# Reading the columns of every 352-column product from last to first

## What is computed

```python
def trunk(x, b_conv, b_h, c_conv, p):
    for l in range(DEPTH):                      # DEPTH = 2
        hn = rmsnorm(x, p['norm_mix_pre'][l])
        if l % 2 == 0:
            m, v, bc, bh = mixer_even(hn, ...)  # h @ w_in (1024 x 2048), gating, LRU, @ w_out (1024 x 1024)
        else:
            m, cc = mixer_odd(hn, ...)          # h @ w_in (1024 x 3072), convolution, @ w_out (1024 x 1024)
        x = x + rmsnorm(m, p['norm_mix_post'][l])
        hn = rmsnorm(x, p['norm_ffn_pre'][l])
        f = jnp.square(jax.nn.relu(hn @ p['mlp_up'][l])) @ p['mlp_down'][l]
        x = x + rmsnorm(f, p['norm_ffn_post'][l])
```

## Time and profile before

| | |
|---|---|
| Three runs | 2157.94 us median (2157.59 to 2158.12) |
| Profiled execution, first to last instruction (its span) | 2155.1 us, mean granted clock 0.999 |
| TensorE (PE) busy | 2146.0 us, 13,496 records |
| Weight loads (PEld) busy | 2135.0 us, 13,496 records |
| VectorE (DVE) busy | 908.0 us |
| ScalarE (ACT) busy | 652.9 us |
| GpSimd (POOL) busy | 100.1 us |

### The profile page before, as it was taken

How to read it: one execution, slowest core, us unless ns; L and a number is a source line. 1 busy time by engine, 2 the same in 40 slices (tenths; PEclk the granted TensorE clock), 3 DMA queues, 4 the chain that set the end, 5 groups by cost and what they waited for, 6 DMA issues and landing times.

```text
span 2155.1 us, 31488 instructions
## 1 busy us (share of the span) xinstructions
PE 2146.0 (100%) x13496; PEld 2135.0 (99%) x13496; DVE 908.0 (42%) x1414; ACT 652.9 (30%) x1105; POOL 100.1 (5%) x127
## 2 busy tenths in 40 slices
PE   9999999999999999999999999999999999999998
PEld 9999999999999999999999999999999999999998
DVE  8766367323322322334953333493223223322336
ACT  6673355202301310333511112453013103202332
POOL 2000000000000000000043231000000000000000
PEclk9999999999999999999999999999999999999999
DMA  5111422111111111141311114222111111111142
GB/s 165 35 41 40 139 88 72 50 40 49 50 42 47 49 50 40 49 135 44 120 50 47 43 50 139 67 84 59 42 48 50 49 40 50 50 42 48 50 140 81
DMA packets 208410, 138.65 MB, mean 64 GB/s; under 512 B 6000, under 2 KB 204784, under 8 KB 208272
## 3 DMA queue, kind: packets, MB, share of 16 engines
q1 hardware_dynamic: 207552, 135.51, 20.6%
q10 hardware_dynamic: 720, 1.13, 0.1%
HBM read 119.22 MB, written 17.40 MB: 63 GB/s over the span
## 4 chain that ended last, share of the span: by engine, by line
PE 99%; ACT 1%; DMA 0%; DVE 0%; issue 0%; DVEq 0%; ACTq 0%
PE ps L698 32%; PE ps L700 32%; PE ps L699 32%; PE ps L773 1%; PE ps L801 0%; PE ps L729 0%; PE ps L720 0%; DMA w_all_raw<-in_w_in_even_dram 0%; PE ps L716 0%; PE ps L784 0%; PE ps L760 0%; ACT L1074 0%; ACT L1030 0%; ACT lru L1030 0%; ACT lru L1032 0%; ACT gelu L1074 0%
## 5 line engine op out<-in xcount | busy, mean ns | idle before, releaser
L698 PE MATMUL ps<-x_hi,w_all 128*128 128x352 f32 x2304 | 747.0, 324 | 0.0
L700 PE MATMUL ps<-x_hi,w_all 128*128 128x352 f32 x2304 | 739.1, 321 | 0.0
L699 PE MATMUL ps<-x_lo,w_all 128*128 128x352 f32 x2304 | 739.1, 321 | 0.0
L698 PE MATMUL ps<-h_hi,w_all 128*128 128x352 f32 x1728 | 556.2, 322 | 0.0
L700 PE MATMUL ps<-h_hi,w_all 128*128 128x352 f32 x1728 | 555.2, 321 | 0.0
L699 PE MATMUL ps<-h_lo,w_all 128*128 128x352 f32 x1728 | 555.2, 321 | 0.0
L698 PEld LDWEIGHTS ps<-x_hi,w_all 128*128 128x128 f32 x2304 | 432.4, 188 | 2.7
L699 PEld LDWEIGHTS ps<-x_lo,w_all 128*128 128x128 f32 x2304 | 432.4, 188 | 2.2
L700 PEld LDWEIGHTS ps<-x_hi,w_all 128*128 128x128 f32 x2304 | 432.3, 188 | 0.0
L876 ACT CAST w_all<-w_all_raw 128x1024 fp32r<-128x1024 f32 x166 | 173.5, 1045 | 525.1 <-DMA w_all_raw<-in_mlp_down_dram 324.8
L698 PEld LDWEIGHTS ps<-h_hi,w_all 128*128 128x128 f32 x1728 | 324.5, 188 | 0.3 <-DVE h_lo L1452 0.3
(11 more groups left out here) (201 smaller groups left out, 1416.0 us busy)
## 6 DMA issues: line engine op xcount, KB each, us to landing
w_all_raw<-in_mlp_up_dram SPq DMA_DIRECT2D x60, 512.0 KB, 3.9
w_all_raw<-in_mlp_down_dram SPq DMA_DIRECT2D x60, 512.0 KB, 3.8
x_save<-f SPq DMA_DIRECT2D x9, 1408.0 KB, 6.0
x_old<-x_save SPq DMA_DIRECT2D x9, 1408.0 KB, 11.5
w_all_raw<-in_c_w_in_dram SPq DMA_DIRECT2D x22, 512.0 KB, 3.7
w_all_raw<-in_w_in_even_dram SPq DMA_DIRECT2D x12, 512.0 KB, 3.6
x_old<-in_x_cols_dram SPq DMA_DIRECT2D x3, 1408.0 KB, 12.8
w_all_raw<-in_w_out_even_dram SPq DMA_DIRECT2D x6, 512.0 KB, 3.8
```

Source lines behind the costliest of these rows:

```text
L698: nc.tensor.matmul(dst, wh, hi, start=(i == 0), stop=False)
L699: nc.tensor.matmul(dst, wh, lo, start=False, stop=False)
L700: last = nc.tensor.matmul(dst, wl, hi, start=False, stop=(i == KC - 1))
```

## The change

A helper `product` replaces the calls of `nc.tensor.matmul` for all 352-column products of the units. It hands the same three operands over, but the output and the moving operand as views that run from the last column to the first. The weights are read as before. The warm-up matmuls, the gate products, the spatial products, transposes and column sums keep their direction. Since both sides are reversed, every column's sum lands where it did. The lists of instructions of all engines, with their waits, are the same as before; only line numbers differ (all products now stand on one line).

```diff
+            def product(out, w, x, start, stop):
+
+                return nc.tensor.matmul(out[:, ::-1], w, x[:, ::-1], start=start, stop=stop)
+
...
-                    nc.tensor.matmul(dst, wh, hi, start=(i == 0), stop=False)
-                    nc.tensor.matmul(dst, wh, lo, start=False, stop=False)
-                    last = nc.tensor.matmul(dst, wl, hi, start=False, stop=(i == KC - 1))
+                    product(dst, wh, hi, i == 0, False)
+                    product(dst, wh, lo, False, False)
+                    last = product(dst, wl, hi, False, i == KC - 1)
...
-                    nc.tensor.matmul(bank(n), w_k(n, 0, k), pt(x_hi, k, 0), start=(k == 0), stop=False)
+                    product(bank(n), w_k(n, 0, k), pt(x_hi, k, 0), k == 0, False)
...
-                    nc.tensor.matmul(bank(n), w_k(n, 0, k), pt(x_lo, k, 0), start=False, stop=False)
+                    product(bank(n), w_k(n, 0, k), pt(x_lo, k, 0), False, False)
...
-                    last = nc.tensor.matmul(bank(n), w_k(n, 1, k), pt(x_hi, k, 0), start=False, stop=(k == KC - 1))
+                    last = product(bank(n), w_k(n, 1, k), pt(x_hi, k, 0), False, k == KC - 1)
```

## The result

| | before | after |
|---|---|---|
| Median | 2158.03 us (2157.59 to 2159.05, 4 runs) | 2186.86 us (2186.83 to 2187.03, 4 runs) |
| Ratio | | 1.0133 (95% interval 1.0119 to 1.0148) |
| Span of the profiled execution | 2155.1 us | 2185.0 us |
| TensorE records | 13,496 | 13,496 |

A forecast was written before the change was run, and what follows sets the result against it. The prediction took TensorE's back-to-back products to bound the kernel. All terms of the change were 0, leaving the span at 2155.1 us and the forecast at the median, 2157.9 us; the range was 2135 to 2270 us.

The forecast's parts named there:

- What bounds the kernel: TensorE, busy 2146.0 of 2155.1 us: 13,248 products at 158.5 ns make 2100 us, so any nanosecond per product reaches the end.
- the 10 ns above the columns: In each 158.3 ns product, columns want about 148 ns; about 10 ns more come from how columns and weight loads meet.
- (a): Instructions on all engines: none added, removed or moved, with semaphores, waits and DMAs as before; cost 0.
- (b): Work behind the products: VectorE and ScalarE take whole units after the last product, so column order doesn't matter; cover not touched.
- (c): Dependences between products of a unit: column 351 is written first and added onto first, so the distance stays one product; cost 0.
- Part (d): The products' read and write at step -1: the sequence of 128-byte halves is unchanged, so the value taken is 0.
- the half-by-half argument: Moving columns of a tile: read downward, its 1408 bytes pass the halves of 256 bytes in the same sequence; nothing changes.
- the streams meet worse: Rival: reversed columns meet weight loads worse inside 128 bytes; 2177 us at 160.0 ns, 2268 us at 166.7 ns; chance 0.19.
- Half speed: Rival: products' downward reads or writes aren't recognised as contiguous, so neighbouring columns no longer share an access; 3990 us, chance 0.13.
- The rule of two independent read ports: Skill page's rule for TensorE: weight loads take no bandwidth from a running matmul; by it reversal costs nothing.

The follow-up runs named there:

- blocks_down: Changed kernel, but with eleven blocks of 32 columns (128 bytes) taken last to first on both sides, upward inside each block: 2158.06 us.
- quads_down: Changed kernel, but with 88 blocks of 4 columns (16 bytes) taken last to first on both sides, upward inside each block: 2187.09 us.
- write_only: Changed kernel, but with the moving columns read upward and only the results written from last to first: 2158.04 us.
- fwd_pad64: Kernel before the change, with 64 bytes of padding ahead of w_all in place of 128: 2172.7 us.
- quads_inside_down: Changed kernel, but with 88 blocks of 4 columns (16 bytes) taken upward on both sides, last to first inside each block: 2158.26 us.

## Why the prediction was wrong

- *What bounds the kernel* was right: 13,248 products back to back, and nothing hides a nanosecond of them. The units' losses in the timelines add up to 29.8 us, and the span grew by 29.9.
- *That the 10 ns above the columns come from the meeting with the weight loads, and depend on place* was right for the part that varies: moving the weights takes the upward pace from 158.3 to 160.0 ns. That all of the 10 ns come from there was not tested, since no run leaves the weight loads out. That these are two reads meeting in the same part of SBUF is the likely reading; the runs show the dependence, not the mechanism.
- *Parts (a), (b), (c)*, each at 0, were right: no engine has a new wait, and the reversed write is free (2158.04 us).
- *Part (d) is the step that failed.* The prediction took the grain at which the trace happened to show placement, 128 bytes, for the grain at which it matters, showed that the sequence of halves is unchanged, and concluded 0. Measured, the term is 28.8 us, 2.2 ns a product. blocks_down confirms the half-by-half argument exactly, at 2158.06 us; quads_down shows what it left out: the order of 16-byte pieces inside, 29.1 us over the kernel before beside it. The trace before had no operand shifted by less than 128 bytes, and the text said so, but under a rival at 0.19 and not as the reason to doubt the central value.
- *The rival "the streams meet worse"* is what happened. Its first price, 19 us with 469 units at 160.0 ns, is close to what those units lost to that step. It missed two terms: tile 1 of h went up a step too, to a pace of 162.2 ns that no row of before shows (3.7 us in 72 units), and 132 units fell into the second pace at 162.1 ns (12.1 us instead of 5.3 at 0.040 us each). With both its 19 us become some 29, against 29.9 in the span.
- *Half speed* was excluded, on both sides: neither the read nor the write passes its columns at half the rate. The Trainium skill's rule on PSUM ("SBUF — State Buffer", same section as cited above) calls any non-contiguous pattern slow; a step of -1 in write_only, at 2158.04 us, is not.
- *The rule of two independent read ports* (the Trainium skill, "TensorE: Matmul & The Clock Gate", the section cited above) was rightly doubted: moving the weights alone changed the time of the kernel before from 2158 to 2173 us (fwd_pad64) and that of the changed kernel by 11 us down or 12 us up.

## What to carry to other kernels

When products run back to back with a weight load beside each, the pace depends on where the moving columns and the weights lie against each other, and on the order in which pieces down to 16 bytes are read; between the best and the worst combination tried here lie 158.3 and 180.0 ns for identical work. Measure the distance from start to start by operand and tile: if it has more than one value, placement is worth trying, and no argument from symmetry is safe below the finest shift that has been measured. A reversed read is not slow in itself, and the place that is best for an upward read need not be the best for another order.

## What was unexpected of the hardware

- The same products at the same places can have two stable paces. Downward they are 160.0 and 162.1 ns, and a single 11-column product switches to the slower one for 23 units, about 90 us. Upward they are 158.3 and 166.7 ns, and one and the same unit took either in different executions; the second was seen in few units, and what chooses it is open.
- The order of reading sets the pace without any simple grain: 64-byte blocks downward 163.3 ns, downward inside 64-byte blocks 180.0 ns, both together at 128 bytes 160.0 ns. (Read and write were both in that order.)
- Writing to PSUM from last to first had no price, for all 352 columns (write_only), for blocks of 32 columns (blocks_down) and within 4 columns (quads_inside_down).

No version tried beats the kernel before. Reversing the order of the weights' columns as well was not tried, nor was an upward read with the weights 16, 32 or 48 bytes past the columns.
